# Loading the input rows of a streaming encoder in groups, norming them as rows inside the first projection, and awaiting a store of values one stage later

## The reference

```python
def rms_norm(x, gain):
    xf = x.astype(jnp.float32)
    y = xf * lax.rsqrt(jnp.mean(xf * xf, axis=-1, keepdims=True) + NORM_EPS)
    return (y * gain.astype(jnp.float32)).astype(x.dtype)
...
h = rms_norm(x, p['norm_mix'][layer])
q, k, v = jnp.split(h @ p['sb_w_qkv'][j], 3, axis=-1)
sb_k_rows.append(k)
sb_v_rows.append(v)
o = stick_breaking_attention(q, k, v, past_len)
```

## Time and profile before

| what | value |
|---|---|
| median of 3 runs | 2262.87 us (2257.93 to 2268.18) |
| the profiled execution's own time | 2263.7 us |
| its span, first to last instruction | 2261.8 us |
| mean granted clock of TensorE | 0.968 |
| PE busy | 2120.5 us, 94% of the span |
| DVE busy | 1215.5 us, 54% |
| ACT busy | 529.5 us, 23% |
| POOL busy | 188.1 us, 8% |
| DMA | 169.82 MB, mean 75 GB/s |

### The profile page before, as it was taken

The page is one execution under the profiler, slowest core; times in us unless marked ns, Lnnn a source line. Parts: engine busy times, 40 slices in busy tenths (PEclk is TensorE's granted clock), DMA queues, the critical chain, the costliest instruction groups (busy, mean ns, idle before and its releaser), DMA issues. The chain is left out here.

```text
span 2261.8 us, 49127 instructions
## 1 busy us (share of the span) xinstructions
PE 2120.5 (94%) x21828; PEld 2011.1 (89%) x21828; DVE 1215.5 (54%) x1705; ACT 529.5 (23%) x968; POOL 188.1 (8%) x249
## 2 busy tenths in 40 slices
PE   6996998997999999996999899998998899999997
PEld 5996768995899999994989899997997699999997
DVE  5333776553656556336558444445653465555434
ACT  2002775112220110001238222224221221011000
POOL 3000000101100000010000322210011010000010
PEclk9998999998999999998999999997999999999998
DMA  3233111451122322322221000004341032232221
GB/s 99 83 124 123 57 48 57 122 151 64 57 84 85 91 83 84 91 86 59 75 67 46 8 4 4 4 4 133 112 152 54 20 89 88 83 90 86 85 85 65
DMA packets 299299, 169.82 MB, mean 75 GB/s; under 512 B 10264, under 2 KB 294112, under 8 KB 299136
## 3 DMA queue, kind: packets, MB, share of 16 engines
q1 hardware_dynamic: 294624, 151.15, 23.1%
q10 hardware_dynamic: 4512, 16.22, 1.9%
HBM read 155.94 MB, written 11.41 MB: 74 GB/s over the span
## 5 line engine op out<-in xcount | busy, mean ns | idle before, releaser
L259 PE MATMUL psum<-words_r,weights_high_r 128*128 128x272 f32 (+1 forms) x7808 | 1497.3, 292 | 13.7 <-DVE words_r L210 13.2
L259 PEld LDWEIGHTS psum<-words_r,weights_high_r 128*128 128x128 f32 x7808 | 1233.9, 190 | 23.9 <-issue 11.6
L259 PE MATMUL psum<-words_r,weight_ring_r 128*128 128x272 f32 (+1 forms) x3904 | 1129.9, 289 | 0.0
L259 PEld LDWEIGHTS psum<-words_r,weight_ring_r 128*128 128x128 f32 x3904 | 740.1, 190 | 0.0
L205 DVE TENSOR_SCALAR weights_high_r<-weight_ring 128x1024 fp32r<-128x1024 f32 (+1 forms) x258 | 177.1, 686 | 523.5 <-PE psum L259 515.1
L210 DVE TENSOR_TENSOR weight_ring_r<-weight_ring,weights_high_r 128x1024 fp32r<-128x1024 f32 (+1 forms) x264 | 319.3, 1209 | 11.2 <-ACT weights_high_r L344 2.4
L399 POOL TENSOR_TENSOR words<-words,words 128x544 f32<-128x544 f32 x42 | 74.6, 1777 | 1282.5 <-ACT words L386 1282.5
L2304 PE MATMUL psum<-words 64*64 64x64 f32 (+1 forms) x3536 | 138.7, 231 | 0.6
L1641 ACT ACTIVATE words<-words 128x544 f32<-128x544 f32 x44 | 29.0, 658 | 454.8 <-DVE words L1584 454.8
L2304 PEld LDWEIGHTS psum<-words 64*64 64x64 f32 x3536 | 129.1, 135 | 3.0 <-DVE words L2227 1.8
L210 DVE TENSOR_TENSOR words_r<-words,words_r 128x544 fp32r<-128x544 f32 (+5 forms) x148 | 104.5, 722 | 6.2 <-ACT words_r L1221 2.6
(11 more groups left out here) (307 smaller groups left out, 1969.7 us busy)
## 6 DMA issues: line engine op xcount, KB each, us to landing
weight_ring<-in_ffn_w_gate_up_dram SPq DMA_DIRECT2D x88, 512.0 KB, 3.8
weight_ring<-in_xa_w_kv_dram SPq DMA_DIRECT2D x32, 512.0 KB, 3.9
weight_ring<-in_ffn_w_down_dram SPq DMA_DIRECT2D x32, 448.0 KB, 3.7
weight_ring<-in_sb_w_qkv_dram SPq DMA_DIRECT2D x24, 512.0 KB, 3.9
weight_ring<-in_xa_w_q_dram SPq DMA_DIRECT2D x16, 512.0 KB, 4.2
weight_ring<-in_xa_w_o_dram SPq DMA_DIRECT2D x16, 512.0 KB, 4.1
weight_ring<-in_ffn_w_down_dram SPq DMA_DIRECT2D x16, 512.0 KB, 4.0
weight_ring<-in_sb_w_o_dram SPq DMA_DIRECT2D x8, 512.0 KB, 4.1
```

The lines of the kernel that those rows point to most:

```text
L259: last = nc.tensor.matmul(c.psum[0:job.m(u), job.bank(q) + h, 0:w], weights[:, k, :], x[:, k, h * w:(h + 1) * w], start=job.opens(u) and k ...
```

## The change

`load_rows`, `load_turned`, `vector_rows`, `stack_vectors` and `turn_vectors` are gone, and three stages with them. Two classes, `Rows` and `Vectors`, take their place, and their work is called from `constants` and from `project_qkv`:

- x is loaded in five pieces on ACT's queue (four of 512 KB, one of 128 KB), each with a semaphore. The first seven vector loads go to SP's queue in `constants`, the other seven to SP at the start of `project_qkv`. The first four weight loads follow there: unit 0 after x's third piece has landed, units 1 to 3 after the fifth.
- PE transposes each piece as it lands, and then the vectors; DVE copies both.
- ACT squares the rows as they were loaded, with the sum along the row taken by the same instruction. The inverse root (Ln, Exp) is then one number for each row. GpSimd multiplies the identity by it, one 128x128 diagonal for each piece; after unit 0 PE multiplies ones by the five diagonals, which spreads the inverse roots over all partitions, and ACT copies them out of PSUM.
- ACT makes the high half straight from x and the gain (Identity with a scale), DVE the low half in one instruction.
- The stores of keys and values get a semaphore each. The projection ends with a wait for the keys' alone; the values' are awaited at the end of SP's program in `stick_breaking`.
- The activation table is loaded in front of `project_qkv` instead of in front of `stick_breaking`; the wait for the padded queries moves behind the other score matmuls of x.

```diff
 def constants(c, rows, vectors):
...
         @block.scalar
         def _(act):
-            loads(act)
+            rows.load(act)
+
+        @block.sync
+        def _(sp):
+            vectors.load(sp, 0, 7)
...
+class Rows:
+    def load(self, act):
+        for m, src in enumerate(self.sources):
+            act.dma_start(self.stage[0:src.shape[0], m, :], src).then_inc(self.landed[m], 16)
+    def turn(self, pe, i):
+        m, k = self.fills[i]
+        w = self.sources[m].shape[0]
+        pe.wait_ge(self.landed[m], 16)
+        if i >= 6:
+            pe.wait_ge(self.copied, i - 5)
+        for j in range(4):
+            last = self.c.nc.tensor.transpose(self.bank(i)[:, j * P:j * P + w], self.stage[0:w, m, (k + j) * P:(k + j + 1) * P], self.c.ident[0:w, 0:w])
+        last.then_inc(self.turned, 1)
+    def square(self, act, m):
...
+        self.c.nc.scalar.activation(self.junk[0:w, :], self.stage[0:w, m, :], ACT.Square, accum_out=self.total[0:w, m:m + 1]).then_inc(self.squared, 1)
+    def take_high(self, act, gain, k):
+        act.wait_ge(self.copied, len(self.fills) - (1 if k < 4 else 0))
+        self.c.nc.scalar.activation(self.high_part[:, k, :], self.x[:, k, :], ACT.Identity, scale=gain[:, k:k + 1]).then_inc(self.high, 1)
+    def take_low(self, dve, gain, k):
+        dve.wait_ge(self.high, k + 1)
+        self.c.nc.vector.scalar_tensor_tensor(out=self.low_part[:, k, :], in0=self.x[:, k, :], scalar=gain[:, k:k + 1],
+                                              in1=self.high_part[:, k, :].bitcast(F32), op0=ALU.mult, op1=ALU.subtract).then_inc(self.low, 1)
+    def invert(self, act):
+        act.wait_ge(self.squared, len(self.sources))
+        nc.scalar.activation(self.root, self.total, ACT.Ln, scale=1.0 / D, bias=self.c.eps[:, 0:1]).then_inc(self.rooted, 1)
+        act.wait_ge(self.rooted, 1)
+        nc.scalar.activation(self.inv_rows, self.root, ACT.Exp, scale=-0.5).then_inc(self.inverted, 1)
+    def make_diagonals(self, pool):
+        pool.wait_ge(self.inverted, 1)
+        for m in range(len(self.sources)):
+            self.c.nc.gpsimd.tensor_scalar(self.diag[:, m, :], self.c.ident[:], self.inv_rows[:, m:m + 1], None, ALU.mult).then_inc(self.spread, 1)
+    def spread_inverse(self, pe):
+        pe.wait_ge(self.spread, len(self.sources))
+        for m, src in enumerate(self.sources):
...
+            last = c.nc.tensor.matmul(c.psum[:, 6 + m // 4, (m % 4) * P:(m % 4) * P + w], c.ones[0:w, :], self.diag[0:w, m, 0:w],
+                                      start=True, stop=True, skip_group_check=True)
...
 def project_qkv(c, job, nxt, x_rows, vectors, qkv, ...):
+    nc.scalar.preload_act_table_set("natural_log_exp_and_others")
         def _(sp):
+            vectors.load(sp, 7, None)
+            for m, units in ((2, (0,)), (4, (1, 2, 3))):
+                sp.wait_ge(x_rows.landed[m], 16)
+                for u in units:
+                    load_unit(c, sp, job, 0, u)
             stream_weights(c, sp, job, nxt)
             past_loads(sp)
-            sp.wait_ge(stored, 4 * 16)
+            sp.wait_ge(k_stored, 2 * 16)
         def _(pe):
-            norm.tensor(pe)
+            for i in range(len(x_rows.fills)):
+                x_rows.turn(pe, i)
+            vectors.turn(pe, 0)
+            pe.wait_ge(vectors.copied, 1)
             for u in range(job.per):
-                multiply_unit(c, pe, job, 0, u, norm.low if u == 0 else None)
+                multiply_unit(c, pe, job, 0, u, x_rows.low if u == 0 else None)
+                if u == 0:
+                    x_rows.spread_inverse(pe)
         def _(pool):
...
+            x_rows.make_diagonals(pool)
             by_pool(pool)
         def _(dve):
+            for i in range(len(x_rows.fills)):
+                x_rows.copy(dve, i)
+            vectors.copy(dve, 0)
+            split_unit(c, dve, job, 0, 0)
+            dve.wait_ge(vectors.copied, 1)
+            for k in range(KT):
+                x_rows.take_low(dve, gain, k)
+            split_unit(c, dve, job, 0, 1)
+            dve.wait_ge(x_rows.ready, 2)
+            for u in range(AHEAD, job.per + AHEAD):
...
         def _(act):
-            norm.scalar(act)
             act.wait_ge(cleared, 1)
+            for m in range(len(x_rows.sources)):
+                x_rows.square(act, m)
+            act.wait_ge(vectors.copied, 1)
+            for k in range(KT):
+                x_rows.take_high(act, gain, k)
+            x_rows.invert(act)
+            x_rows.copy_inverse(act)
...
 def stick_breaking(c, q, k, v_rows, v_new, past, o, spaces, v_stored):
-    nc.scalar.preload_act_table_set("natural_log_exp_and_others")
...
                 past.load_v(sp, p)
+            sp.wait_ge(v_stored, 2 * 16)
...
-                else:
-                    pe.wait_ge(queries_padded, 2)
...
+                if p == 0:
+                    pe.wait_ge(queries_padded, 2)
                 mm(zs["x0"][0:DEC, NEW_AT:], k[:, p, SEQ:T], q_new[:, p, :], start=False, stop=False, skip_group_check=True).then_inc(scored["x"], 1)
```

More of the change, by code:

```diff
@@ L606, in same_block, with constants @@
         self.keep(pool, v, [[w, P // w], [0, w]], ALU.is_ge, w - 1, -1)
-def constants(c, loads):
+def constants(c, rows, vectors):
     nc = c.nc
@@ L681, in wkv_constants @@
     return make
[L684 to L704, removed]
@@ L707, in turn_vectors @@
[L707 to L722, removed]
@@ L725, in load_rows @@
[L725 to L769, removed]
@@ new lines, with __init__, load, turn @@
+class Vectors:
+    def __init__(self, c):
+        self.c = c
+        self.stack = [c.flat(5, P), c.flat(5, P, at=P)[0:56, :]]
+        self.landed, self.turned, self.copied = c.nc.alloc_semaphore("vectors_landed"), c.sem("vectors_turned"), c.sem("vectors_copied")
+        c.columns = c.tile("vector_columns", [P, P + 56])
+        c.vec, self.loads = {}, []
+        for t, rows, base in ((self.stack[0], ROWS_A, 0), (self.stack[1], ROWS_B, P)):
+            at = 0
+            for name, k in rows:
+                src = c.ins[name]
+                dims = " ".join(f"d{i}" for i in range(len(src.shape)))
+                self.loads.append((t[at:at + k, :], src.rearrange(f"{dims} -> ({dims})").rearrange("(k p) -> k p", p=P)))
+                c.vec[name] = c.columns[:, base + at:base + at + k]
+                at += k
+    def load(self, sp, first, end):
+        for dst, src in self.loads[first:end]:
+            sp.dma_start(dst, src).then_inc(self.landed, 16)
+    def turn(self, pe, bank):
+        c = self.c
+        pe.wait_ge(self.landed, 16 * len(self.loads))
+        c.nc.tensor.transpose(c.psum[:, bank, 0:P], self.stack[0], c.ident[:])
+        c.nc.tensor.transpose(c.psum[:, bank, P:P + 56], self.stack[1], c.ident[0:56, 0:56]).then_inc(self.turned, 1)
+    def copy(self, dve, bank):
+        dve.wait_ge(self.turned, 1)
+        self.c.nc.vector.tensor_copy(self.c.columns[:], self.c.psum[:, bank, 0:P + 56]).then_inc(self.copied, 1)
@@ L780, with project_qkv @@
 UNIT_BANK = dict(x0=0, y0=2, x1=3, y1=5, s=6)
-def project_qkv(c, job, nxt, norm, qkv, k_rows, v_rows, k_new, v_new, by_pool, past_loads, stored):
+def project_qkv(c, job, nxt, x_rows, vectors, qkv, k_rows, v_rows, k_new, v_new, by_pool, past_loads, k_stored, v_stored):
     nc, outs = c.nc, c.outs
@@ L831, in _ @@
         def _(dve):
-            for u in range(job.per + AHEAD):
+            for i in range(len(x_rows.fills)):
[8 more added lines that the diff above has]
+            for u in range(AHEAD, job.per + AHEAD):
                 if u < job.per:
                     split_unit(c, dve, job, 0, u)
-                if u == 0:
-                    norm.vector(dve)
-                    norm.mean(dve)
-                if u == 1:
-                    norm.invert(dve)
                 v = u - AHEAD
-                if v >= 0:
-                    dve.wait_ge(*done(c, job, v))
-                    nc.vector.tensor_tensor(halves(qkv[:, target(v):target(v) + 1, :]), psum_of(c, job, v), norm.inverse(),
-                                            ALU.mult).then_inc(c.slot_emptied[job.slot(v)], 1)
+                dve.wait_ge(*done(c, job, v))
+                nc.vector.tensor_tensor(halves(qkv[:, target(v):target(v) + 1, :]), psum_of(c, job, v), x_rows.inverse(),
+                                        ALU.mult).then_inc(c.slot_emptied[job.slot(v)], 1)
         @block.scalar
         def _(act):
-            norm.scalar(act)
             act.wait_ge(cleared, 1)
+            for m in range(len(x_rows.sources)):
[5 more added lines that the diff above has]
+            x_rows.copy_inverse(act)
+            act.wait_ge(cleared, 2)
             for f in range(groups * tiles):
```

68 lines of the change are left out of this document (48 added, 20 removed).

## The result

The changed kernel took 2234.98 us (median of 4 runs, 2233.87 to 2235.25) beside 2265.52 us for the kernel before (4 runs, 2257.93 to 2268.21): a ratio of 0.987, 95% interval 0.9843 to 0.9896. That is 30.5 us less; the forecast was 2236 us, 26.7 less on the profiled execution. The changed kernel's own profiled execution took 2233.87 us, 29.8 less than the 2263.7 of before.

The account below looks back on a forecast made before the run. PE, busy 94% of the span, was taken to leave time only where idle: the start (16.4 us) and the seam between projection and stick-breaking (10.3). Together 26.7 us gave 2236 us, range 2228 to 2244.

Parts of the forecast that it names:

- Loads and turning: Start: last small vector load lands at 12.1 us as before (lower bound 10.9), vectors copied at 13.24.
- The turning of x: Start: eight wide copies at 0.69 us each, all ten ended at about 11 us, hidden behind the vectors.
- Halves: Start: VectorE's eight low halves at 0.77 us each, ended at about 20.7; ACT's high halves at 0.64, always ahead.
- The rival with 1.89 each: Start: low halves take 1.89 us, unit 1 starts at 32.3, gain 9.9 instead of 16.4, 2242.7 us; chance 0.12.
- The five diagonals: Start, new chain on the path: GpSimd takes 5.8 us, until 25.0; five matmuls add 0.8, unit 1 at 25.8.
- The clock: Start: PE pauses only from about 13 to 16; a fallen clock costs unit 0 up to 2 us, overall nothing or 1.
- The pause of 2 to 3 us behind unit 0: Sign of being right: PE pauses 2 to 3 us after unit 0, ending with GpSimd, unit 1 at 25 to 26.
- The seam: Projection to stick-breaking: without the wait for stored values, 10.3 us gained; bounds 8.0 and 11.4, up to 2 more.
- The two meet: Seam: keys' landing allows the first copy at 202.3, the chain from the cap wants it at 201.7 to 203.6; 203.5 taken.
- The sum: Whole kernel: start 16.4 plus seam 10.3 gives 26.7 us gained, 2236 us against the median.
- The rival in which the stage's end waits for DMAs: Seam doesn't open, as the stage's end awaits outstanding DMAs anyway; only the start remains, 2246 us; chance 0.03.
- the slower one: Projection: granted clock stays at 0.50, each unit costs 6.05 us more; eight such units give 2284 us; chance 0.02.

Follow-up runs that it names:

- e7: Changed kernel with three unused matmuls of ones in PE's pause before unit 0 and the five diagonals made by VectorE, not GpSimd: 2237.63 us, ratio 0.989.
- e11: Changed kernel with the past keys loaded before the weights' stream and three unused matmuls of ones in PE's pause before unit 0: 2233.0 us, ratio 0.9866.
- e6: Changed kernel with the five diagonals made by VectorE between the low halves and the split of unit 1, not by GpSimd: 2237.24 us, ratio 0.9901.
- e1: Changed kernel with the projection's end awaiting the store of values again: 2241.8 us, ratio 0.9905.
- e10: Changed kernel with nothing edited, run again for more times and a second profile: 2232.05 us, ratio 0.9863.
- e5: Changed kernel with three unused matmuls of ones in PE's pause between the turned vectors and unit 0: 2230.66 us, ratio 0.9866.
- e3: Changed kernel with the two loads of past keys issued before the projection's stream of weights: 2228.7 us, ratio 0.9859.

## Why the prediction was right

**Loads and turning.** The small vectors no longer set the time here. I had kept 12.1 for their landing with 10.9 as the bound; PE turned them at 11.54, and was free of x's turning only then (in e7 and e11 it waited for the last of them until 11.7). The turning of x was under-sized: I took the 0.69 us of VectorE's copies, but the first six were paced by PE at 0.85, and the last ended at 12.3, where I had 11. The two errors met by luck: vectors copied at 12.6, forecast 13.2.

**Halves.** 0.78 us each, forecast 0.77, but started 0.70 apart, so done at 20.0 (forecast 20.7). The rival with 1.89 each was not seen. GpSimd was at rest only until 18.38; beside its diagonals the last three low halves still took no more than 0.81. The diagonals did suffer, as the view of line L793 shows, whole and from 21 us on:

```profile
L793 POOL TENSOR_SCALAR words<-ident,words x5: 598/1334/1363, 18.4 to 22.9; 128x128 f32<-128x128 f32 x5
...
L793 POOL TENSOR_SCALAR words<-ident,words x3: 598/599/1363, 21.0 to 22.9; 128x128 f32<-128x128 f32 x3
```

The five diagonals took 5.16 us, forecast 5.8, but not evenly: up to 1.36 us each while VectorE was at its halves and splits, 0.60 once it was idle. The Trainium skill's GPSIMD Engine Reference (section 4.1, Engine selection) has one-input work run at roughly line rate. The trace doesn't agree, even at 0.60: the same five took 1.06 us together on VectorE (e6). With the 0.29 of the earlier trace rows for each the chain would have been under a third as long.

**The clock.** Here the forecast was off, with no harm. I said that the granted clock might hold over PE's pause of 3 us, and that unit 0 would end at 22.1, with 24.1 if not, either ahead of the diagonals at 25.0. It did fall; unit 0 took 8.4 us for 6.05 and ended at 23.66, the diagonals at 23.54, so in this profile unit 0 ends the wait and not the diagonals that I called the path. The pause of 2 to 3 us behind unit 0 that I named as a sign is not there (0.5 us in e1 and e10, 2.0 in e5). The spread behind it took 1.35 us for the 0.8 that I had from the transposes. Unit 1 started at 25.0, forecast 25.8: 17.2 us gained for 16.4.

**The seam.** 9.1 us at the barrier (forecast 8.7). The cap came 2.8 us behind the stage's start, within the 2.3 to 4.2. The keys landed 11.1 us behind their issue, as read from the earlier trace rows. The Trainium skill's page DMA: Bandwidth & Descriptors (section Anatomy of one DMA) fits its 2.0 us plus bytes at 436 GB/s to transfers that GpSimd issues. For this one, issued by SP, that makes an estimated 3.2 us, which is far off beside the store, and under the 3.9 that a weight load of this size took with no store beside it. The copy gained 10.9, forecast 10.3, with 11.4 as the bound. "The two meet" held: the landing put the changed kernel's copy 1.0 us back (6.87 behind its cap for 5.85 in e3), and in e10, where the scores took longer (2.93 us for 1.59, at the low clock), the copy followed its cap by 5.84 us.

**The sum.** 17.2 + 10.9 = 28.1 at the first pair's copy, where I had 26.7 (28.2 as read directly). Behind it, in code that the change leaves alone, 3.7 us went in the first stretch of the table, 1.3 and 4.2 came in the other two, and 0.4 went behind them: 29.6 in the spans. I had given the seam up to 2 us more if the clock stayed high behind it, where it was low, and nothing for the rest of the program. That these nearly cancel is luck: the second profiles of both kernels lie 36.7 us apart. The range of 2228 to 2244 held the result with room for that, as the spread of the first three runs had been added to it.

The rival in which the stage's end waits for DMAs fell with e1 (9.4 us at the barrier), and the slower one with the clock at 1.00 from 21 us to the projection's end.

## What to carry to other kernels

A profile shows one releaser for a wait; before taking it away, look for what ends next, and by how much. Here unit 0 at the low clock and the diagonals ended 0.1 us apart, so either edit alone brought unit 1 forward by 0.3 us, and both by 1.9. And when local gains of 2 us are wanted in a kernel whose runs differ by 10, measure them between two instructions in the profile: the median of the edit that was best at its place was 7 us above that of one that gained nothing there.

## What was not expected

The same instructions of the same kernel took 12.4 or 16.1 us behind the first copy, from one profile to the other, as TensorE's granted clock was at 0.50 for 3.4 us or 12.3 of it. Layer 1's cross attention took 57.0, 61.1 or 63.2 us among kernels that don't differ in it, with 6.8, 17.1 and 20.5 us at the low clock. One 128x128 operation on GpSimd took 0.60 us with VectorE idle and 1.36 beside it, while VectorE's own instructions were not slowed (0.78 to 0.81).
